# Differential attention in a diffusion block: scores as alternating matmuls on the upper and lower 64 rows, three passes each, keys in two parts

## The chip, the cores and the metric

The kernel runs on one core of a Trainium2 chip. The metric is the device time of one execution in microseconds (us); each version is timed several times and the median is quoted.

## What is computed

The reference is one layer of a diffusion block on 1024 latent tokens with 256 context tokens: an input projection, three parallel branches (differential attention, pooling, windowed attention), their merge, and a feed-forward part. Only the differential attention is touched. It has 4 heads, and each head has two sub-heads `s` with queries and keys of 64 features (q of 1024 tokens, k of 1280):

```python
s = jnp.einsum('bqhsd,bkhsd->bhsqk', qblk, k).astype(jnp.float32) * scale
p = jax.nn.softmax(s, axis=-1)
a = p[:, :, 0] - lam * p[:, :, 1]
return jnp.einsum('bhqk,bkhe->bqhe', a.astype(v.dtype), v)
```

The kernel keeps float32 accuracy by cutting each operand into a high part that fits the matmul's reduced type and a low remainder. A product is then the sum of the products of parts.

## The kernel before

The program is a row of stages with barriers: `prepare`, `project`, `features`, `diff` (the differential attention), `window`, `merge`, `residual`, `ffn_in`, `ffn_out`. The change touches `diff`, and in `features` only the early load of head 0.

`project` leaves, per head, four stacks in DRAM (`stacks_da`), q of sub-head 0, q of sub-head 1, k of sub-head 0, k of sub-head 1, each of 128 rows: 64 rows of high parts above 64 rows of low parts. `load_head` (L776) brings a head on SP's queue with five DMAs: `q_st` and `k_st` as they lie, `k_sw` with its two halves swapped, and `val`. `features` issues it for head 0 (L586), `diff` for the other three.

`diff` runs a hardware loop over two pairs of heads. A turn of the loop (`it`) has 16 tiles of 128 queries (8 for each head of the pair), so there are 32 tiles, and 19 steps, because the tail of a tile's work is done up to three steps later (LAG_TURN 2, LAG_AV 3). PSUM banks 0 to 2 hold the scores of sub-head 0, banks 3 to 5 those of sub-head 1, without a second buffer; banks 6 and 7 form a ring for transposes and products. Every engine has its order written out:

- PE, step i: `scores(i)` (L868), the transposes of the "last" two key blocks of tile i-2, the `products` with the values of tile i-3 (L888), then the transposes "low" and "high" of tile i-2 (L881). In `scores`, sub-head s first waits for `exp_done[s]` of tile i-1, since that exp reads the banks which are now overwritten. Each of its three column pieces (512, 512, 256) takes two matmuls over all 128 rows: q stack by `k_st`, which gives high by high and low by low, and q stack by `k_sw`, which gives the two mixed products. `sc_done[s]` goes up after each sub-head's six.
- DVE (VectorE): `maximum` of sub-head 0 and of sub-head 1 (L981, L982), `combine` of tile i-1 (L996), then the reciprocals, which wait for both exps of tile i.
- ACT (ScalarE): exp of sub-head 0 (L927), `copy_last` (L943, L946), which waits for the products, exp of sub-head 1, two copies "low" and "high" (L934), and a sum of squares (L956). `copy_last` frees the bank into which PE writes the "high" transposes.

Of the kernel before, what the change touches and what calls it, by code (L numbers as in the profile page):

```python
# [34 lines left out]
F32 = mybir.dt.float32  # L35
F32R = mybir.dt.float32r
# [5 lines left out]
P = 128  # L42
D = 1024
SEQ = 1024
CTX = 256
TOK = SEQ + CTX
KC = D // P
TL = SEQ // P
TT = TOK // P
# [5 lines left out]
HD = 64  # L55
# [441 lines left out]
def features(nc, sem, banks, io, keep):  # L497
# [11 lines left out]
    with ExitStack() as ctx:  # L509
        sb = lambda n, s, d=F32: ctx.enter_context(nc.sbuf_tensor(n, s, d))  # L510
# [28 lines left out]
        @block.sync  # L539
        def _(sp):  # L540
            for dst, src in ((pw, io["pool_w"]), (pscale, io["pool_scaleT"]), (badaT, io["b_adaT"]), (ngT, io["norm_gT"])):
                sp.dma_start(dst[:], src).then_inc(small_in, 16)

            def load_w(f, slot):
                sp.wait_ge(w_lo_ready, f - 1)
                sp.dma_start(w_raw[slot][:], io["w_feat"][f]).then_inc(w_in[slot], 16)

            def load_piece(q, slot):
                sp.wait_ge(piece_used, q + 1)
                sp.dma_start(piece[slot][:], io["w_ada"].rearrange("(k p) n -> p k n", p=P)  # L550
                             .rearrange("p k (a n) -> a p k n", n=AC)[2 * D // AC + q]).then_inc(piece_in[slot], 16)

            def store_gate(f):
                for n in range(NH):
                    sp.wait_ge(gst_ready, (f - G) * NH + n + 1)
                    sp.dma_start(gates[f - G][:, n * HALF:(n + 1) * HALF], gst[n][:]).then_inc(gst_out[n], 16)

            for g in range(G):
                if g:
                    sp.wait_ge(pooled, g)  # L560
                sp.dma_start(inv, io["inv_count"][g:g + 1, :].to_broadcast([P, SEQ])).then_inc(inv_in, 16)
                load_w(g + 2, g % 2)
                if g >= 1:
                    sp.wait_ge(yb_ready, g)
                    sp.dma_start(io["yb"][g - 1], yb[:]).then_inc(yb_out, 16)

            def turn(it, pieces, more):
                for j in range(2):
                    f = it * 2 + G + j
                    if more:  # L570
                        load_w(f + 2, j)
                    for q in range(2 * pieces):
                        load_piece((it - 1) * 4 + 2 * j + q, q)
                    store_gate(f)

            load_w(G + 2, 0)
            sp.wait_ge(yb_ready, G)
            sp.dma_start(io["yb"][G - 1], yb[:]).then_inc(yb_out, 16)
            store_gate(G)
            load_w(G + 3, 1)  # L580
            store_gate(G + 1)
            with sp.Fori(1, 1 + A_TURNS) as it:
                turn(it, 1, True)
            with sp.Fori(1 + A_TURNS, TURNS - 1) as it:
                turn(it, 0, True)
            load_head(io, sp, 0, keep["head0"], keep["head0_in"])  # L586
            sp.wait_ge(ada_ready, 1)
            for i in range(2):
                if i:
                    sp.wait_ge(row_used, 2)  # L590
                sp.dma_start(brow, io["b_ada"][0:1, (2 + 3 * i) * D:(3 + 3 * i) * D].to_broadcast([P, D])).then_inc(row_in, 16)
                sp.dma_start(grow, io["norm_g"][1 + 2 * i:2 + 2 * i, :].to_broadcast([P, D])).then_inc(row_in, 16)
            turn(TURNS - 1, 0, False)
            sp.wait_ge(row_used, 3)
            sp.dma_start(io["late_row"], upad[0:1, 0:D]).then_inc(yb_out, 16)
            for j in range(2):
                sp.wait_ge(keep["st_out"][j], keep["st_stored"])
            for n in range(NH):
                sp.wait_ge(gst_out[n], 16 * (3 * KC + 1))
            sp.wait_ge(yb_out, 16 * (G + 1))  # L600
# [174 lines left out]

def load_head(io, sp, h, buffers, landed):  # L776

    q, k, ks, val = buffers
    src = io["stacks_da"][h]
    for dst, s in ((q[:], src[0:2, :, 0:SEQ]), (k[:], src[2:4])):  # L780
        sp.dma_start(dst.bitcast(F32), s.rearrange("s p n -> p s n")).then_inc(landed, 16)
    for a, b in ((0, HD), (HD, 0)):
        sp.dma_start(ks[a:a + HD].bitcast(F32), src[2:4, b:b + HD].rearrange("s p n -> p s n")).then_inc(landed, 16)
    sp.dma_start(val[:], io["vals"][h].rearrange("t p n -> p t n")).then_inc(landed, 16)


def window_buffers(keep):
# [20 lines left out]
def diff(nc, sem, banks, io, keep):  # L808
# [4 lines left out]
    TILES = 2 * TL  # L813
    LAG_TURN, LAG_AV = 2, 3
    COLS = [(0, HALF), (HALF, HALF), (2 * HALF, TOK - 2 * HALF)]
    with ExitStack() as ctx:
        sb = lambda n, s, d=F32: ctx.enter_context(nc.sbuf_tensor(n, s, d))

        heads = [keep["head0"], (sb("q_st1", [P, 2, SEQ], F32R), sb("k_st1", [P, 2, TOK], F32R), sb("k_sw1", [P, 2, TOK], F32R),
                                 sb("val1", [P, TT, P]))]  # L820
        q_st, k_st, k_sw, val = zip(*heads)
        e = [[sb(f"e{b}{s}", [P, TOK]) for s in range(2)] for b in range(2)]
        a = [sb(f"a{b}", [P, TOK]) for b in range(2)]
        at = [sb(f"at{b}", [P, TT, P]) for b in range(2)]
# [7 lines left out]
        sc_done, neg_ready, exp_done = ([sem(f"da_{n}{s}") for s in range(2)] for n in ("sc", "neg", "exp"))  # L832
# [12 lines left out]
        def slot(it, i, what):  # L845

            n = 3 * (i - LAG_TURN) + RING.index(what)
            return n % 2, it * USES + n // 2
# [12 lines left out]
        @block.tensor  # L861
        def _(pe):
            def use(it, i, what):
                b, used = slot(it, i, what)
                pe.wait_ge(free[b], used + 1)
                return b, banks[6 + b]

            def scores(it, i):  # L868
                j, t = i // TL, i % TL
                if t == 0:  # L870
                    pe.wait_ge(head_in[j], 80 * it + 80)
                for s in range(2):
                    pe.wait_ge(exp_done[s], it * TILES + i + 1)
                    q = q_st[j][:, s, t * P:(t + 1) * P]
                    for c, (c0, w) in enumerate(COLS):
                        out = banks[3 * s + c][:, 0:w]
                        pe.matmul(out, q, k_st[j][:, s, c0:c0 + w], start=True, stop=False)
                        mm = pe.matmul(out, q, k_sw[j][:, s, c0:c0 + w], start=False, stop=True)  # L878
                    mm.then_inc(sc_done[s], 1)

            def turn(it, t, i, what):  # L881

                b, bank = use(it, i, what)
                for n, k in enumerate(KEYS[what]):
                    mm = pe.transpose(bank[:, n * P:(n + 1) * P], a[t % 2][:, k * P:(k + 1) * P], ident[:])
                return b, mm

            def products(t, bank):  # L888
                for k in range(TT):
                    mm = pe.matmul(bank[:, 2 * P:3 * P], at[t % 2][:, k, :], val[t // TL][:, k, :], start=(k == 0), stop=(k == TT - 1))  # L890
                return mm

            with pe.Fori(0, 2) as it:
                for i in range(STEPS):
                    t = i - LAG_TURN
                    if i < TILES:
                        scores(it, i)
                    if t >= 0:
                        if t < TILES:
                            pe.wait_ge(a_ready, it * TILES + t + 3)  # L900
                            b, mm = turn(it, t, i, "last")
                        else:
                            b, bank = use(it, i, "last")
                        if t >= 1:
                            for what in ("low", "high"):
                                bb, used = slot(it, i - 1, what)
                                pe.wait_ge(free[bb], used + 2)
                            mm = products(t - 1, banks[6 + b])
                            mm.then_inc(av_done, 1)
                            pe.wait_ge(av_done, it * TILES + t)  # L910
                            pe.sem_inc(turned[b], 1)
                        else:
                            mm.then_inc(turned[b], 1)
                    if 0 <= t < TILES:
                        for what in ("low", "high"):
                            b, mm = turn(it, t, i, what)
                            mm.then_inc(turned[b], 1)
                pe.sem_inc(turned[slot(it, STEPS - 1, "low")[0]], 1)
# [1138 lines left out]
```

## Time and profile before

| | us |
|---|---|
| median of 3 executions | 2089.27 |
| lowest and highest | 2085.03, 2089.52 |
| span of the profiled execution | 2084.4 |
| `diff` in it, first score matmul to last product | 679.0 to about 907 |

The profiled execution is one more execution; its span runs from its first to its last instruction, and no other time of it is given. Times in the trace count from the span's start. A row of the timeline has the start, the duration, engine, line, operation, tiles and shapes, a count where equal instructions are merged, and in brackets the idle time before it and what ended it. The granted clock of TensorE (PEclk) is 1.00 at 2.4 GHz and 0.50 at 1.2 GHz. Matmuls overlap, so their pace is read from start to start and not from their durations. PEld is the weight load, which runs beside the matmuls.

### The profile page before, as it was taken

The numbers are of one execution on the slowest core, as the hardware profiler recorded it, in microseconds if no ns is written. First come the engines' busy times: TensorE is split into PE (matmuls) and PEld (weight loads), VectorE is DVE, ScalarE is ACT, GpSimd is POOL, SyncE is SP. The second block draws the span as 40 slices with busy tenths as digits, with TensorE's granted clock in tenths as the row PEclk, the third lists the DMA queues.
The fourth block names the chain that finished last, engine by engine and source line by source line (L and its number), as shares of the span: only waits on it lengthen the run. The fifth ranks groups of instructions, "written<-read, shape, count | busy, mean of one in ns | idle before, by whom it ended". The sixth has DMA issues, their size and how long they took to land. (4 is left out here: it accounts for less than half of the span.)

```text
span 2084.4 us, 28313 instructions
## 1 busy us (share of the span) xinstructions
PE 1951.4 (94%) x10084; PEld 1665.9 (80%) x10084; DVE 855.8 (41%) x1526; ACT 661.1 (32%) x1218; POOL 390.4 (19%) x209
## 2 busy tenths in 40 slices
PE   6799999999999898979899989799999999989998
PEld 2699998788887787869887878688888888878886
DVE  2755554736531786858673346500000000032322
ACT  2422222122221675755451025411111111132332
POOL 0321120222221000020001212122222222133433
PEclk9799999999999999999899999899999999999999
DMA  9133322266655333220204342211111111143431
GB/s 327 61 100 96 105 82 87 104 189 191 188 155 182 84 84 83 65 81 2 72 0 152 136 164 84 81 41 50 50 50 43 47 50 50 40 152 100 162 111 71
DMA packets 132934, 207.17 MB, mean 99 GB/s; under 512 B 10881, under 2 KB 93441, under 8 KB 132098
## 3 DMA queue, kind: packets, MB, share of 16 engines
q1 hardware_dynamic: 132866, 206.31, 30.4%
q8 instruction: 37, 0.61, 0.1%
q14 instruction: 31, 0.25, 0.0%
HBM read 164.99 MB, written 41.29 MB: 99 GB/s over the span
## 5 line engine op out<-in xcount | busy, mean ns | idle before, releaser
L490 PE MATMUL psum<-h_hi,cut_hi 128*128 128x512 f32 x704 | 275.0, 391 | 6.1 <-DVEq L1716 6.1
L491 PE MATMUL psum<-h_lo,cut_hi 128*128 128x512 f32 x704 | 274.6, 390 | 0.0
L493 PE MATMUL psum<-h_hi,cut_lo 128*128 128x512 f32 x704 | 217.2, 390 | 0.0
L1723 DVE TENSOR_TENSOR f<-psum,i_act 128x512 f32 x44 | 28.4, 687 | 454.7 <-PE psum L493 454.7
L490 PE MATMUL psum<-h_hi,f_hi 128*128 128x512 f32 x448 | 177.7, 397 | 2.3 <-ACTq L668 2.3
L491 PE MATMUL psum<-h_lo,f_hi 128*128 128x512 f32 x448 | 175.9, 393 | 0.0
L1704 POOL TENSOR_TENSOR cut_lo<-stage,cut_hi 128x1024 fp32r<-128x1024 f32 x42 | 100.7, 2397 | 367.5 <-ACT cut_hi L1683 367.5
L76 PE MATMUL psum<-w_hi,h_hi 128*128 128x384 f32 (+1 forms) x464 | 156.7, 338 | 5.7 <-DVE w_lo L431 5.6
L490 PEld LDWEIGHTS psum<-h_hi,cut_hi 128*128 128x128 f32 x704 | 132.6, 188 | 34.0 <-DVEq L1715 6.5
L491 PEld LDWEIGHTS psum<-h_lo,cut_hi 128*128 128x128 f32 x704 | 132.7, 189 | 27.6
L493 PEld LDWEIGHTS psum<-h_hi,cut_lo 128*128 128x128 f32 x704 | 132.5, 188 | 27.7
L78 PE MATMUL psum<-w_hi,h_lo 128*128 128x384 f32 (+1 forms) x464 | 151.8, 327 | 0.0
L77 PE MATMUL psum<-w_lo,h_hi 128*128 128x384 f32 (+1 forms) x464 | 151.7, 327 | 0.0
L76 PE MATMUL psum<-u_hi,uf_hi 128*128 128x512 f32 x352 | 138.3, 393 | 5.9 <-POOL uf_lo L1871 5.6
L493 PE MATMUL psum<-h_hi,f_lo 128*128 128x512 f32 x448 | 138.7, 391 | 0.0
L77 PE MATMUL psum<-u_lo,uf_hi 128*128 128x512 f32 x352 | 137.9, 392 | 0.0
L78 PE MATMUL psum<-u_hi,uf_lo 128*128 128x512 f32 x352 | 137.9, 392 | 0.0
L1888 DVE TENSOR_TENSOR u_lo<-stage,u_hi 128x1024 fp32r<-128x1024 f32 x44 | 58.4, 1330 | 157.6 <-ACT u_hi L1849 157.6
L697 POOL TENSOR_TENSOR f_lo<-f_raw,f_hi 128x1024 fp32r<-128x1024 f32 x26 | 65.2, 2507 | 267.7 <-ACT f_hi L657 267.7
L1871 POOL TENSOR_TENSOR uf_lo<-f,uf_hi 128x512 fp32r<-128x512 f32 x44 | 78.4, 1787 | 156.1 <-ACT uf_hi L1850 156.1
L981 DVE TENSOR_REDUCE mx<-psum 128x1 f32<-128x1280 f32 x64 | 95.2, 1487 | 21.7 <-PE psum L878 19.2
L1683 ACT ACTIVATE cut_hi<-stage 128x1024 fp32r<-128x1024 f32 x42 | 44.6, 1063 | 187.0 <-PE psum L493 187.0
(232 smaller groups left out, 3839.5 us busy)
## 6 DMA issues: line engine op xcount, KB each, us to landing
stage<-in_w_ff SPq DMA_DIRECT2D x44, 512.0 KB, 3.3
stage<-in_w_ffn_out SPq DMA_DIRECT2D x44, 512.0 KB, 3.3
piece<-in_w_ada SPq DMA_DIRECT2D x32, 512.0 KB, 5.6
f_raw<-in_w_feat SPq DMA_DIRECT2D x28, 512.0 KB, 4.3
gates_dram<-gst SPq DMA_DIRECT2D x48, 256.0 KB, 2.1
b_g<-gates_dram SPq DMA_DIRECT2D x8, 1536.0 KB, 7.9
w_raw<-in_w_tok SPq DMA_DIRECT2D x6, 1536.0 KB, 6.7
ada<-in_w_ada SPq DMA_DIRECT2D x8, 1024.0 KB, 11.4
```

The source lines that it names most:

```text
L76: pe.matmul(out, sh, mh, start=first, stop=False)
L77: pe.matmul(out, sh, ml, start=False, stop=False)
L78: return pe.matmul(out, sl, mh, start=False, stop=last)
L490: pe.matmul(out, sh, mh, start=first, stop=False)
L491: pe.matmul(out, sh, ml, start=False, stop=False)
L493: mm = pe.matmul(out, sl, mh, start=False, stop=last)
L697: eng.tensor_tensor(w_lo[slot][:], w_raw[slot][:], w_hi[slot][:].bitcast(F32), ALU.subtract).then_inc(w_lo_ready, 1)
L981: ch.link(v.tensor_reduce(mx[:, s:s + 1], psum[:, 3 * s * HALF:3 * s * HALF + TOK], AX.X, ALU.max))
L1683: act.activation(w_hi[slot][:], w_raw[slot], ACT.Copy).then_inc(w_hi_ready, 1)
L1704: eng.tensor_tensor(w_lo[slot][:], w_raw[slot], w_hi[slot][:].bitcast(F32), ALU.subtract).then_inc(w_lo_ready, 1)
L1871: nc.gpsimd.tensor_tensor(f_lo[j][:], f[:, k, c * HALF:(c + 1) * HALF], f_hi[j][:].bitcast(F32), ALU.subtract).then_inc(f_lo_ready, 1)
L1888: v.tensor_tensor(w_lo[j][:], w_raw[(q + c * FC) % 2][:], w_hi[j][:].bitcast(F32), ALU.subtract)\
```

## The change

The k_sw stack goes. q and k are loaded so that rows 0 to 63 hold sub-head 0 and rows 64 to 127 sub-head 1, and the high and low parts lie side by side in the middle dimension. `load_head` still has five DMAs, each of the q and k ones over 64 rows. A score is now three matmuls of 64 rows (high by high, high by low, low by high; low by low is no longer computed). The two sub-heads alternate from matmul to matmul, each on its own half of the rows and into its own banks. That makes 18 matmuls for a tile in place of 12. Both waits, for `exp_done[0]` and `exp_done[1]` of the tile before, stand ahead of the first of them, and `sc_done[0]` goes up with the last but one, `sc_done[1]` with the last.

```diff
--- before.py
+++ after.py
@@ -583,7 +583,7 @@
                 turn(it, 1, True)
             with sp.Fori(1 + A_TURNS, TURNS - 1) as it:
                 turn(it, 0, True)
-            load_head(io, sp, 0, keep["head0"], keep["head0_in"])
+            load_head(io, sp, 0, head0_buffers(keep), keep["head0_in"])
             sp.wait_ge(ada_ready, 1)
             for i in range(2):
                 if i:
@@ -775,13 +775,19 @@
 
 def load_head(io, sp, h, buffers, landed):
 
-    q, k, ks, val = buffers
-    src = io["stacks_da"][h]
-    for dst, s in ((q[:], src[0:2, :, 0:SEQ]), (k[:], src[2:4])):
-        sp.dma_start(dst.bitcast(F32), s.rearrange("s p n -> p s n")).then_inc(landed, 16)
-    for a, b in ((0, HD), (HD, 0)):
-        sp.dma_start(ks[a:a + HD].bitcast(F32), src[2:4, b:b + HD].rearrange("s p n -> p s n")).then_inc(landed, 16)
+    q, k, val = buffers
+    src = io["stacks_da"][h].rearrange("u (x d) n -> u d x n", x=2)
+    for s in range(2):
+        rows = slice(s * HD, (s + 1) * HD)
+        sp.dma_start(q[rows].bitcast(F32), src[s, :, :, 0:SEQ]).then_inc(landed, 16)
+        sp.dma_start(k[rows].bitcast(F32), src[2 + s]).then_inc(landed, 16)
     sp.dma_start(val[:], io["vals"][h].rearrange("t p n -> p t n")).then_inc(landed, 16)
+
+
+def head0_buffers(keep):
+
+    q, k, ks, val = keep["head0"]
+    return q, k, val
 
 
 def window_buffers(keep):
@@ -813,12 +819,12 @@
     TILES = 2 * TL
     LAG_TURN, LAG_AV = 2, 3
     COLS = [(0, HALF), (HALF, HALF), (2 * HALF, TOK - 2 * HALF)]
+    PARTS = [(0, 0), (0, 1), (1, 0)]
     with ExitStack() as ctx:
         sb = lambda n, s, d=F32: ctx.enter_context(nc.sbuf_tensor(n, s, d))
 
-        heads = [keep["head0"], (sb("q_st1", [P, 2, SEQ], F32R), sb("k_st1", [P, 2, TOK], F32R), sb("k_sw1", [P, 2, TOK], F32R),
-                                 sb("val1", [P, TT, P]))]
-        q_st, k_st, k_sw, val = zip(*heads)
+        heads = [head0_buffers(keep), (sb("q_st1", [P, 2, SEQ], F32R), sb("k_st1", [P, 2, TOK], F32R), sb("val1", [P, TT, P]))]
+        q_st, k_st, val = zip(*heads)
         e = [[sb(f"e{b}{s}", [P, TOK]) for s in range(2)] for b in range(2)]
         a = [sb(f"a{b}", [P, TOK]) for b in range(2)]
         at = [sb(f"at{b}", [P, TT, P]) for b in range(2)]
@@ -871,12 +877,16 @@
                     pe.wait_ge(head_in[j], 80 * it + 80)
                 for s in range(2):
                     pe.wait_ge(exp_done[s], it * TILES + i + 1)
-                    q = q_st[j][:, s, t * P:(t + 1) * P]
-                    for c, (c0, w) in enumerate(COLS):
-                        out = banks[3 * s + c][:, 0:w]
-                        pe.matmul(out, q, k_st[j][:, s, c0:c0 + w], start=True, stop=False)
-                        mm = pe.matmul(out, q, k_sw[j][:, s, c0:c0 + w], start=False, stop=True)
-                    mm.then_inc(sc_done[s], 1)
+
+
+                for c, (c0, w) in enumerate(COLS):
+                    for n, (a, b) in enumerate(PARTS):
+                        for s in range(2):
+                            rows = slice(s * HD, (s + 1) * HD)
+                            mm = pe.matmul(banks[3 * s + c][:, 0:w], q_st[j][rows, a, t * P:(t + 1) * P],
+                                           k_st[j][rows, b, c0:c0 + w], start=n == 0, stop=n == len(PARTS) - 1)
+                            if c == len(COLS) - 1 and n == len(PARTS) - 1:
+                                mm.then_inc(sc_done[s], 1)
 
             def turn(it, t, i, what):
```

## Rows read from the trace of the kernel before

**Rows 1.** The page: the span and TensorE's share of it.

```profile
span 2084.4 us, 28313 instructions
PE 1951.4 (94%) x10084; PEld 1665.9 (80%) x10084; DVE 855.8 (41%) x1526; ACT 661.1 (32%) x1218; POOL 390.4 (19%) x209
```

**Rows 2.** Timeline of PE, one steady step of the attention.

```profile
741.24 0.48 PE L877 MATMUL psum<-k_st,q_st 128*128 128x512 f32 x1
741.56 0.39 PE L878 MATMUL psum<-k_sw,q_st 128*128 128x512 f32 x1
...
742.26 0.28 PE L877 MATMUL psum<-k_st,q_st 128*128 128x256 f32 x1
742.37 0.27 PE L878 MATMUL psum<-k_sw,q_st 128*128 128x256 f32 x1
...
743.51 0.28 PE L878 MATMUL psum<-k_sw,q_st 128*128 128x256 f32 x1
...
743.85 2.40 PE L890 MATMUL psum<-val,at 128*128 128x128 f32 x20
746.40 1.43 PE L885 MATMUL psum<-ident,a 128*128 128x128 f32 x8
747.58 0.48 PE L877 MATMUL psum<-k_st,q_st 128*128 128x512 f32 x1
```

**Rows 3.** Timeline of DVE, the same step.

```profile
742.75 1.49 DVE L981 TENSOR_REDUCE mx<-psum 128x1 f32<-128x1280 f32 x1
...
744.35 1.48 DVE L981 TENSOR_REDUCE mx<-psum 128x1 f32<-128x1280 f32 x1
```

**Rows 4.** Timeline of ACT, the same step.

```profile
744.47 1.33 ACT L927 ACTIVATE e<-psum,neg_m 128x1280 f32<-128x1280 f32 x1 [1.11 <-DVE neg_m L982]
745.70 0.19 ACT L927 ACTIVATION_READ_ACCUMULATOR e<-psum,neg_m 128x1 f32 x1
746.47 0.37 ACT L943 ACTIVATE o<-psum,rec 128x128 f32 x1 [0.58 <-PEq L911]
...
747.00 1.33 ACT L927 ACTIVATE e<-psum,neg_m 128x1280 f32<-128x1280 f32 x1
748.22 0.21 ACT L927 ACTIVATION_READ_ACCUMULATOR e<-psum,neg_m 128x1 f32 x1
```

**Rows 5.** Timeline of ACT: the first and last exp of sub-head 0 in either turn.

```profile
683.25 1.33 ACT L927 ACTIVATE e<-psum,neg_m 128x1280 f32<-128x1280 f32 x1 [0.39 <-DVE neg_m L982]
...
776.19 1.33 ACT L927 ACTIVATE e<-psum,neg_m 128x1280 f32<-128x1280 f32 x1 [1.11 <-DVE neg_m L982]
...
797.41 1.33 ACT L927 ACTIVATE e<-psum,neg_m 128x1280 f32<-128x1280 f32 x1 [0.40 <-DVE neg_m L982]
...
889.88 1.33 ACT L927 ACTIVATE e<-psum,neg_m 128x1280 f32<-128x1280 f32 x1 [1.11 <-DVE neg_m L982]
```

**Rows 6.** Timeline of PE, the first tile of all.

```profile
679.00 0.79 PE L877 MATMUL psum<-k_st,q_st 128*128 128x512 f32 x1 [5.14 <-ACTq L961]
...
680.01 0.63 PE L877 MATMUL psum<-k_st,q_st 128*128 128x512 f32 x1
680.44 0.63 PE L878 MATMUL psum<-k_sw,q_st 128*128 128x512 f32 x1
```

**Rows 7.** Busy time by stretch: columns PE, PEld, DVE, ACT, POOL, PEclk, DMA share, GB/s.

```profile
684.72:690.60 5.88, 4.26 (x12) 3.33 (x12) 4.15 (x8) 2.84 (x4) 0.00 (x0) 0.69 1.04 270
690.60:696.00 5.40, 3.51 (x18) 2.72 (x18) 5.04 (x7) 2.80 (x5) 0.00 (x0) 1.00 0.81 168
798.90:804.20 5.30, 2.83 (x12) 2.08 (x12) 3.60 (x7) 2.84 (x4) 0.00 (x0) 1.00 1.05 289
804.20:809.80 5.60, 4.80 (x18) 3.85 (x18) 5.04 (x7) 2.86 (x5) 0.00 (x0) 0.70 1.06 215
744.47:750.81 6.34, 6.04 (x44) 5.30 (x44) 5.19 (x8) 4.64 (x11) 0.00 (x0) 1.00 0.55 181
```

**Rows 8.** Timeline of DVE, the end of the features stage.

```profile
673.96 1.23 DVE L772 TENSOR_TENSOR upad<-psum,piece 128x1024 f32<-128x1024 f32 x1 [6.12 <-DMA piece<-in_norm_g]
```

## The prediction

> **What bounds the kernel now.** I read the page first: TensorE (PE) is busy for 94% of 2084.4 us [rows 1], so fewer matmul slots look like time saved. The change lies in the attention only, so I then read one steady step of it in the timelines of PE, DVE and ACT. From score start to score start it lasts 747.58 - 741.24 = 6.34 us [rows 2], and PE is busy in 6.04 of these [rows 7]. The twelve score matmuls run from 741.24 to 743.51 by their starts, the products take 2.40 us from 743.85, ACT's copy follows at 746.47 [rows 4], and it frees the bank for the last transposes before the next scores. So PE's own round, through that one copy, sets the step.
>
> A second loop runs beside it, through the score banks: scores, maximum, exp, and then scores again. Sub-head 0 has its maximum at 742.75, sub-head 1 only at 744.35 [rows 3]; exp 0 starts at 744.47 and exp 1 at 747.00 [rows 4]. The next scores of sub-head 0 start at 747.58, while exp 1 is still running: it ends at 748.22 + 0.21 = 748.43. Today this is harmless. PE does the six matmuls of sub-head 0 first (1.15 us), and comes to sub-head 1 at about 748.7, when exp 1 has ended. The stagger of the two sub-heads hides 0.85 us of exp 1.
>
> **The matmuls.** Removed: twelve of 128 rows; added: eighteen of 64 rows. At full clock the pace of 512 columns is 0.23 us (three in 742.26 - 741.56 = 0.70), that of 256 columns 0.11 (742.37 - 742.26), and the first matmul has 0.32 before its second [rows 2]. No row shows a matmul on 64 rows, so I bound the cost from both sides. If the halves don't overlap, eighteen follow one another: the last of sub-head 0 starts at 0.32 + 11 x 0.23 + 4 x 0.115 = 3.31 us. If each pair shares a slot and the weight loads too, it is 0.32 + 5 x 0.23 + 2 x 0.115 = 1.70. Between lies the case in which pairs overlap and loads don't: the twenty product matmuls have only 128 columns and still take 2.40 / 20 = 0.12 us each [rows 2], the pace of a weight load. Two loads then cost 0.23 for every pair, which fits below 512 columns and not below 256, and the last matmul of sub-head 0 starts at 0.32 + 7 x 0.23 = 1.93 us. I take this one: each half has its own rows and its own banks, which speaks for overlap, and 0.12 us for a load is the nearest row.
>
> The Trainium skill, TensorE: Matmul & The Clock Gate, section Part 3: Packing small matmuls, states that matmuls on different row groups run at the same time, starting about 4 ns apart, and that four row tiles of 512 columns gave 3.07 times the rate. No row of this trace shows it. By the 4 ns the sum stays as it is; by 3.07 out of 4 a pair would cost about 1.3 slots, an estimate that adds some 0.4 us a step to it.
>
> From the start of the last matmul of a sub-head to its maximum it is 742.75 - 742.37 = 0.38 us [rows 2, 3]. Call L the time from the first score matmul to the first maximum: 1.51 us now, 1.93 + 0.38 = 2.31 after (2.08 with shared loads, 3.69 in series). All the slots saved are saved for sub-head 1; sub-head 0 gets its scores later than today.
>
> **The wait that is moved.** `exp_done[1]` of the tile before now stands ahead of all scores. Behind it in PE's order are both sub-heads' scores, the transposes and the products; DVE and ACT wait for these. The loop through the banks becomes:
>
> - L = 2.31 to the first maximum;
> - 744.47 - 742.75 = 1.72 to exp 0 [rows 3, 4];
> - 745.70 + 0.19 - 744.47 = 1.42 for exp 0 with its accumulator read [rows 4];
> - 0.55 for `copy_last` ahead of exp 1, from 747.00 - 746.47 = 0.53 and a small step [rows 4];
> - 748.43 - 747.00 = 1.43 for exp 1, and 0.05 to PE, an estimate from the small gaps of these rows.
>
> Together L + 5.17 = 7.48 us, against 6.34. What else could be late? The products end at about 1.93 + 0.11 + 0.34 + 2.40 = 4.8 us after the step's start and their copy could go at 5.0; exp 0 ends at 2.31 + 3.14 = 5.45, so the products have 0.4 us to spare. The second maximum ends, with its scaling, before `copy_last` is over: DVE is 1.60 us behind its first maximum there [rows 3] and exp 1 could start at L + 3.32, against L + 3.69. ACT's copies and squares after exp 1 are done today 1.11 us before the next exp 0 [rows 4], and that exp comes later relative to them after the change.
>
> In the first two periods of each turn there is no `copy_last`, and maximum 1 opens exp 1: L + 1.72 + 1.60 + 1.43 + 0.05, so L + 4.8 = 7.1; the third is about 7.2.
>
> **Sum at full clock.** A turn has 15 periods between its first and last exp 0: 2 x 7.1 + 7.2 + 12 x 7.48 = 111.2 us, against 776.19 - 683.25 = 92.9 and 889.88 - 797.41 = 92.5 [rows 5]. That is 18.3 + 18.7 = 37.0. The first exp of a turn comes later by the 0.8 of L: + 1.6. The tail gains about 0.4 per turn, since exp 1 follows exp 0 after 1.97 in place of 2.53: - 0.8. Sum + 37.8.
>
> **The clock.** The first tile runs at the 1.2 GHz level: 512 columns take 0.43 us and the first matmul 0.6 [rows 6]. In the second turn the clock is full over two steps in which PE is busy for 2.83 of 5.30 us, and then it is at 0.70 in the next stretch [rows 7], with steps of scores alone before it. After the change such steps have 2.0 us of scores in 7.1, less than there. I take four cold scores in the first turn and two in the second. Cold, L is 0.6 + 7 x 0.43 + 0.6 = 4.2, which is 1.9 more: 6 x 1.9 = 11.4, less 1.0, because the first exp 0 of today was already cold (683.25 - 679.00 = 4.25 [rows 5, 6], where I counted 1.51 + 1.72 plus 0.8). Net + 10.4, with 0 and 16 as bounds. In steady steps PE will be busy for some 5.6 of 7.5 us in gaps below 1 us, and 690.60 to 696.00 had 3.51 of 5.40 at clock 1.00 [rows 7], so there I take the full clock.
>
> **The loads.** `k_sw` of 1.28 MB goes from each head. Heads 1 to 3 have tens of us of cover, the attention steps before their first use. Head 0's load stands in the features stage ahead of row loads for which DVE waited 6.12 us at its end [rows 8]; after that wait only about 2.5 us of DVE and a store are left, next to the last gates, which PE's end holds. I take - 0.5, bounds 0 and - 1. No cover is lost, since nothing is added to SP.
>
> Forecast: 37.8 + 10.4 - 0.5 = + 47.7 on a profiled span of 2084.4, so 2132 as a span. It is 4.9 below the median of 2089.27 in the runs shown; the delta is put on the median: 2137 us.
>
> **The rivals.**
>
> 1. The halves don't overlap, so that the change doesn't do what it says. L is 3.69, the step 8.86: 2 x 8.5 + 8.6 + 12 x 8.86 = 131.9 per turn, + 78.7 for both; + 4.4 for the first exps, - 0.8 for tails, + 6 for the colder start: + 88, so 2177 us. For it: not one row shows an overlap. Against it: separate rows, weights and banks.
> 2. The clock sinks in steady steps too, since PE now rests twice in each step. Cold scores give L = 4.2; the products end at 4.2 + 0.5 + 20 x 0.22 = 9.1 and become the late ones; copy, exp 1 and the way back add 2.0: 11.1 us a step, + 3.6 over the forecast. For 24 steps that is + 87: 2224 us, or half, if it comes and goes. Rows 7 speak against it.
> 3. Faster: the joint wait doesn't bind, and PE's round alone sets the step. It would be 6.34 less 0.34 (2.27 us from first to last score start become 1.93), or less 0.55 with shared loads: 26 steps x 0.34 = - 9, so 2080 us. The place is the wait at the head of `scores`; it decides from L + 5.17 < 6.34, so L below 1.17 us. Nine slots of columns alone need 1.70 + 0.38, so only a shorter chain of maxima and exps could bring it, and every link of that is a measured row.
>
> **How the numbers follow.** Forecast 0.65, series 0.19, clock 0.08, faster 0.04, and 0.04 for a result within 0.2%, if small gains elsewhere pay for the wait. Within the forecast the low end has shared loads (- 7) and no cold start (- 10): 2119. The range runs from there to the series case with its start: 2117 to 2180. A measurement of this kernel can tell about 0.2% from no change. Slower by more than that: 0.92; within: 0.04; faster: 0.04.
>
> **What would show it.** Right: steps of 7.3 to 7.6 us between the exps of sub-head 0, the two maxima back to back with the first some 2.3 us after the scores' start, PE waiting for exp 1 ahead of the first score, and pairs of matmuls of the two halves starting together. The first maximum at 3.7 us after the start would show series; matmuls of 0.63 us in mid-turn would show the clock. The prediction is wrong if the next scores start before exp 1 of the tile before has ended, or if the steps of 6.34 us stay.

## The result and the profile after

The changed kernel takes 2124.79 us (median of 4 runs, 2123.81 to 2127.53), the kernel before 2089.11 beside it: 1.0173 times as long, with a 95% interval of 1.0161 to 1.0186, so + 35.7 us. The forecast was 2137, its range 2117 to 2180. The profiled spans are 2123.8 and 2084.4 us, 39.4 apart.

The page of the changed kernel, its head:

```profile
span 2123.8 us, 28729 instructions
PE 1950.4 (92%) x10276; PEld 1663.6 (78%) x10276; DVE 859.3 (40%) x1526; ACT 656.8 (31%) x1218; POOL 390.2 (18%) x209
```

In the sum PE is busy for as long as before [rows 1], 1950 us: the 39 us more of the span are idle time of PE. The steady step tells where most of them are. Timelines of PE, then DVE, then ACT of the changed kernel:

```profile
746.15 0.63 PE L895 MATMUL psum<-ident,a 128*128 128x128 f32 x4
747.18 0.66 PE L895 MATMUL psum<-ident,a 128*128 128x128 f32 x4 [0.40 <-ACT at L956]
748.58 2.03 PE L886 MATMUL psum<-k_st,q_st 64*128 64x512 f32 x18 [0.74 <-ACT e L937]
750.53 0.44 PE L895 MATMUL psum<-ident,a 128*128 128x128 f32 x2
750.81 2.40 PE L900 MATMUL psum<-val,at 128*128 128x128 f32 x20
```

```profile
750.65 1.49 DVE L991 TENSOR_REDUCE mx<-psum 128x1 f32<-128x1280 f32 x1 [1.64 <-PE psum L886]
752.17 0.15 DVE L992 TENSOR_SCALAR neg_m<-mx 128x1 f32<-128x1 f32 x1
752.24 1.48 DVE L991 TENSOR_REDUCE mx<-psum 128x1 f32<-128x1280 f32 x1
```

```profile
745.18 1.33 ACT L937 ACTIVATE e<-psum,neg_m 128x1280 f32<-128x1280 f32 x1 [2.68 <-DVE neg_m L992]
746.40 0.19 ACT L937 ACTIVATION_READ_ACCUMULATOR e<-psum,neg_m 128x1 f32 x1
746.49 0.36 ACT L953 ACTIVATE o<-psum,rec 128x128 f32 x1
...
747.01 1.34 ACT L937 ACTIVATE e<-psum,neg_m 128x1280 f32<-128x1280 f32 x1
748.22 0.22 ACT L937 ACTIVATION_READ_ACCUMULATOR e<-psum,neg_m 128x1 f32 x1
```

All eighteen score matmuls take 750.53 - 748.58 = 1.95 us, against 743.64 - 741.24 = 2.40 for the twelve of before ([rows 2], and the next row of that timeline):

```profile
743.64 0.38 PE L885 MATMUL psum<-ident,a 128*128 128x128 f32 x2
```

The halves do overlap: read one by one, the pairs of 512 columns start 0.23 us apart and those of 256 columns about 0.11, and the second matmul of a pair starts 0.03 to 0.07 us behind the first. But the scores start only when exp 1 has ended, at 748.44 (the bracket: PE idle for 0.74 us, released by ACT's exp), where [rows 2, 4] had sub-head 0 start 0.85 us before that end. The first maximum comes 2.07 us after the start, in place of 1.51 [rows 2, 3]. ACT, which had 0.58 us to wait for the products ahead of its copy [rows 4], now goes from exp 0 to the copy at once: the products are no longer late, the exps are. The steady step is 7.19 us for 6.34.

The exps of sub-head 0 that answer to [rows 5], from ACT's timeline of the changed kernel:

```profile
683.75 1.33 ACT L937 ACTIVATE e<-psum,neg_m 128x1280 f32<-128x1280 f32 x1 [0.39 <-DVE neg_m L992]
...
795.46 1.33 ACT L937 ACTIVATE e<-psum,neg_m 128x1280 f32<-128x1280 f32 x1 [2.65 <-DVE neg_m L992]
...
818.11 1.33 ACT L937 ACTIVATE e<-psum,neg_m 128x1280 f32<-128x1280 f32 x1 [0.40 <-DVE neg_m L992]
...
929.25 1.33 ACT L937 ACTIVATE e<-psum,neg_m 128x1280 f32<-128x1280 f32 x1 [2.65 <-DVE neg_m L992]
```

Against [rows 5]: + 0.5 at the first, + 18.8 in the first turn (111.7 for 92.9), + 1.4 between the turns (22.65 for 21.22), + 18.7 in the second (111.1 for 92.5). That is 39.4, the whole difference of the spans; all stages behind are as long as before. Of a turn's 18.7, about 10 are twelve steady steps, the rest is the first three periods, which answer to [rows 7] (busy time by stretch, columns as there):

```profile
683.75:692.16 8.41, 3.47 (x18) 2.90 (x18) 3.63 (x7) 2.83 (x4) 0.00 (x0) 0.62 1.04 209
692.16:700.67 8.51, 5.05 (x24) 4.06 (x24) 5.10 (x8) 2.84 (x5) 0.00 (x0) 0.60 0.13 33
700.67:709.15 8.48, 5.99 (x39) 5.20 (x40) 5.09 (x8) 3.98 (x7) 0.00 (x0) 0.80 0.00 0
709.15:716.34 7.19, 5.87 (x51) 5.03 (x50) 5.14 (x8) 4.52 (x10) 0.00 (x0) 1.00 0.01 2
```

They take 8.4 to 8.5 us at a mean clock of 0.60 to 0.80. PE has little but scores in the first two (18 and 24 matmuls), and the scores of all three take 3.5 us in place of 1.95.

### The profile page after: what moved, and what is told of

Its sections match the earlier page's. It is cut to its first block and busy times, and to the rows that moved or that the text cites. A ratio compares the mean times of both kernels' runs of the same rounds, so it can differ in the third digit from the quotient of the medians.

```text
span 2123.8 us, 28729 instructions
## 1 busy us (share of the span) xinstructions
PE 1950.4 (92%) x10276; PEld 1663.6 (78%) x10276; DVE 859.3 (40%) x1526; ACT 656.8 (31%) x1218; POOL 390.2 (18%) x209
## 3 DMA queue, kind: packets, MB, share of 16 engines
q1 hardware_dynamic: 131842, 201.06, 29.7%
## 5 line engine op out<-in xcount | busy, mean ns | idle before, releaser
L886 PE MATMUL psum<-k_st,q_st 64*128 64x512 f32 (+1 forms) x576 | 74.5, 405 | 45.4 <-ACT e L937 38.5
L937 ACT ACTIVATE e<-psum,neg_m 128x1280 f32<-128x1280 f32 x64 | 85.2, 1331 | 95.9 <-DVE neg_m L992 95.9
```

Of the source, the lines that this page charges most:

```text
L886: mm = pe.matmul(banks[3 * s + c][:, 0:w], q_st[j][rows, a, t * P:(t + 1) * P], k_st[j][rows, b, c0:c0 + w], start=n == 0, stop=n == len(P ...
L937: act.activation(e[i % 2][s][:], psum[:, 3 * s * HALF:3 * s * HALF + TOK], ACT.Exp, scale=SCALE, bias=neg_m[:, i % 2, s:s + 1], accum_out= ...
```

## The experiments

The theory is that the joint wait ends the stagger of the two sub-heads and hangs the step on a loop through L, both exps and back, L + 5.11 us by the trace of after. Its rival puts the cost into the matmuls of 64 rows, their number or their loads.

**e1_joint_wait**: the kernel before, with only the wait moved.

```diff
                 for s in range(2):
                     pe.wait_ge(exp_done[s], it * TILES + i + 1)
+                for s in range(2):
                     q = q_st[j][:, s, t * P:(t + 1) * P]
```

> The kernel before with one edit: both exp waits stand ahead of sub-head 0's six matmuls (128 rows, two passes, as before). Theory (the joint wait undoes the stagger): in the step of before exp 1 ends 748.43 - 741.24 = 7.19 us after the scores' start, and products, copy and exp 1 ahead of it don't change, so the step goes from 6.34 to about 7.24 us and the run gains 13 us a turn and some for the cold start, + 25 to + 33 us in all. Rival (the narrow matmuls or their loads cost the time, the wait is covered): steps stay at 6.34, + 0 to + 3 us.

Measured: 1.0162 (1.0143 to 1.0182), 2124.0 against 2090.2 us, steps of 7.34 us. PE's timeline of e1_joint_wait:

```profile
748.67 0.47 PE L878 MATMUL psum<-k_st,q_st 128*128 128x512 f32 x1 [0.74 <-ACT e L928]
748.98 0.39 PE L879 MATMUL psum<-k_sw,q_st 128*128 128x512 f32 x1
```

The same bracket as in the changed kernel, with the old matmuls. The wait alone costs + 34 us, a little over the + 25 to + 33 expected and as much as the whole change within the intervals. The rival's + 0 to + 3 is out. The step is 7.34 and not 7.24 because the way from the end of exp 1 to the first score is 748.67 - (748.31 + 0.21) = 0.15 us, by ACT's timeline, for which I had 0.05.

**e2_alternate_old**: the wait moved and the sub-heads alternating, still two passes of 128 rows.

```diff
-                    for c, (c0, w) in enumerate(COLS):
...
+                for c, (c0, w) in enumerate(COLS):
+                    for n, keys in enumerate((k_st[j], k_sw[j])):
+                        for s in range(2):
+                            mm = pe.matmul(banks[3 * s + c][:, 0:w], q_st[j][:, s, t * P:(t + 1) * P],
+                                           keys[:, s, c0:c0 + w], start=n == 0, stop=n == 1)
...
```

> The kernel before with both waits ahead and the two sub-heads alternating, still with twelve matmuls of 128 rows. Theory: the first maximum waits for the eleventh matmul, so L = 2.16 + 0.38 = 2.54 us, and the bank loop, whose rest was 7.18 - 2.07 = 5.11 in the changed kernel, makes steps of 7.65 us; + 45 to + 55 us, so more than the changed kernel's + 36, because here no pair of matmuls overlaps. Rival (the row halves bring nothing): no slower than the changed kernel, steps of 7.2 or below.

Measured: 1.0266 (1.0247 to 1.0284), + 54 us, steps of 7.65 us, the number of the sum L + 5.11; L is 2.54 in its trace too. So alternation by itself delays sub-head 0 and makes it worse than e1_joint_wait; the eighteen matmuls on halves, which overlap, earn back some 19 us of that (1.0266 to 1.0173).

**e3_blocks**: the new matmuls in the old order, nine of sub-head 0 behind its wait, then nine of sub-head 1 behind its own. e4 to e6 share its code, with another LEAD.

```diff
-                for s in range(2):
-                    pe.wait_ge(exp_done[s], it * TILES + i + 1)
...
+                mine = [(c, n) for c in range(len(COLS)) for n in range(len(PARTS))]
+                LEAD = 9
+                pe.wait_ge(exp_done[0], it * TILES + i + 1)
+                for x in range(len(mine) + LEAD):
+                    if x == LEAD:
+                        pe.wait_ge(exp_done[1], it * TILES + i + 1)
+                    for s, y in enumerate((x, x - LEAD)):
+                        if not 0 <= y < len(mine):
+                            continue
...
```

> The changed kernel's eighteen matmuls of 64 rows, but nine of sub-head 0 behind its own wait and then nine of sub-head 1 behind its own, as the order of before. Theory: a matmul of 64 rows alone takes the slot of one with 128 (0.23 us for 512 columns), so the scores take 3.45 us; PE's round sets the step again, 6.34 + 1.15 = 7.5 us; the stagger is back, and the first maximum comes 2.1 us after the start. + 30 to + 40 us. Rival (a 64-row matmul is cheaper by itself, alternating isn't what overlaps them): scores in about 1.9 us, steps near 6.0, - 5 to - 10 us.

Measured: 1.0193 (1.0172 to 1.0214), + 38 us, steps of 7.38. PE's timeline of e3_blocks, one step:

```profile
745.09 1.43 PE L898 MATMUL psum<-ident,a 128*128 128x128 f32 x8
746.44 3.27 PE L889 MATMUL psum<-k_st,q_st 64*128 64x512 f32 x18
749.64 0.44 PE L898 MATMUL psum<-ident,a 128*128 128x128 f32 x2
```

The same eighteen matmuls take 3.20 us here, near the 3.45 expected for eighteen full slots, and 1.95 when they alternate. A matmul of 64 rows by itself takes nearly the slot of one of 128 rows, and the gain is in the pairing alone. The stagger is back here, but PE's round is longer: ACT waits 0.87 us for the products ahead of its copy.

**e4_lead3, e5_lead2, e6_lead4**: alternating, with sub-head 0 ahead by three, two or four matmuls that need only exp 0 (LEAD = 3, 2, 4).

> The changed kernel, but sub-head 0 leads by three matmuls (its first 512 columns), which wait for exp 0 alone; the wait for exp 1 comes then, and the rest alternates in pairs, sub-head 1 three behind. Theory: exp 1 is awaited 0.78 us into the scores, L is 2.30, so the bank loop gives 2.30 + 5.11 - 0.78 = 6.63 us; PE's round 6.34 + 0.12 = 6.46 lies below it. Steps of 6.6 us, + 8 to + 15 us, so two thirds of the loss of + 36 is given back by order alone. Rival (the cost is in the 64-row matmuls and their loads): steps stay near 7.2, + 30 or more.

> As e4_lead3, with sub-head 0 two matmuls ahead. In e4_lead3 the step was 6.83 us, set by PE's round and not by the bank loop. Theory: the wait for exp 1 now stands 0.55 us into the scores, L about 2.26, so the bank loop gives 2.26 + 5.11 - 0.55 = 6.82; PE's round loses two slots of 0.115 and is about 6.6. Steps of 6.8 us, + 18 to + 24 us, no better than lead 3, with PE now waiting for exp 1 inside the scores. Rival (only the number of slots on PE counts): 6.6 and + 10 to + 15.

> As e4_lead3, with sub-head 0 four matmuls ahead. Theory: PE's round has 0.23 us more than with lead 3, so steps of 7.06 us; the bank loop (2.26 + 5.11 - 1.01 = 6.36) doesn't bind. + 26 to + 32 us. Rival (the bank loop still binds in lead 3, so more lead helps): 6.6 us or less, + 12 to + 16.

| | ratio | 95% interval | steady step, us |
|---|---|---|---|
| changed kernel (no lead) | 1.0173 | 1.0161 to 1.0186 | 7.19 |
| e5_lead2 | 1.0110 | 1.0093 to 1.0126 | 6.83 |
| e4_lead3 | 1.0108 | 1.0090 to 1.0127 | 6.84 |
| e6_lead4 | 1.0118 | 1.0101 to 1.0134 | 6.84 |
| e3_blocks (lead of nine) | 1.0193 | 1.0172 to 1.0214 | 7.38 |

Order alone, with the same matmuls and loads, gives back 13 us, so the theory stands; but two of the three expectations missed. Lead 3 cost + 21 us and not + 8 to + 15, and lead 4 + 24 and not + 26 to + 32, no worse than lead 3 within the intervals. Only lead 2 came as expected, with its step of 6.83 set by the bank loop: ACT goes from exp 0 to the copy at once there, while in lead 3 and 4 it waits 0.15 and 0.32 us for PE's products. I had PE's round too low for lead 3 (6.46) and too high for lead 4 (7.06). The timeline of e4_lead3 shows it:

```profile
747.37 1.43 PE L898 MATMUL psum<-ident,a 128*128 128x128 f32 x8
748.73 2.73 PE L889 MATMUL psum<-k_st,q_st 64*128 64x512 f32 x18
751.39 0.44 PE L898 MATMUL psum<-ident,a 128*128 128x128 f32 x2
751.66 1.06 PE L903 MATMUL psum<-val,at 128*128 128x128 f32 x8
```

Its copy of that step starts at 747.45, so from the copy to the first score it is 1.28 us, where [rows 2, 4] have 747.58 - 746.47 = 1.11; transposes to products take 0.27 where they took 0.21; and the scores take 751.39 - 748.73 = 2.66 where they took 2.40. That is 0.17 + 0.06 + 0.26 = 0.49 on top of 6.34, the step of 6.83; I had counted 0.12. e3_blocks has the same 1.28. The scores take 2.66 us in lead 4 as well. In lead 3 a load among them waits 0.20 us for exp 1; in lead 4 none waits, but one more matmul at either end runs without a partner. None of the three comes near the 6.34 us of before.

**e9_dummy128, e10_dummy64**: is the missing time the way from 128-row to 64-row matmuls? The kernel before gets one small matmul ahead of sub-head 0's scores, whose output they overwrite, on 128 rows (control) or on 64.

```diff
                     q = q_st[j][:, s, t * P:(t + 1) * P]
+                    if s == 0:
+                        pe.matmul(banks[0][:, 0:P], k_st[j][:, 0, 0:P], k_st[j][:, 0, 0:P], start=True, stop=True)
```

(e10_dummy64 has `k_st[j][0:HD, 0, 0:P]` in both places.)

> The kernel before with one added matmul of 128 rows and 128 columns ahead of sub-head 0's scores, whose output is overwritten by them. It is the control of e10_dummy64: its slot is about 0.12 us, PE sets the step, so steps of 6.45 us and + 2 to + 5 us.

> As e9_dummy128, but the added matmul is on 64 rows, with 128-row work on either side. In e3_blocks to e6_lead4 the way from copy_last to the first 64-row score was 1.28 us against 1.11 before, and from the transposes to the products 0.28 against 0.22. Theory (going from 128-row to 64-row matmuls and back costs PE time): steps 0.2 to 0.3 us longer than in e9_dummy128, 6.65 to 6.75, + 9 to + 14 us. Rival (that 0.17 us belongs to the first score's load or its wait, not to the change of rows): the same steps as e9_dummy128.

Measured: e9_dummy128 1.0019 (1.0003 to 1.0034), steps of 6.45 us, as expected; e10_dummy64 1.0094 (1.0066 to 1.0121), + 20 us, steps of 6.80; both lie above what was expected, + 9 to + 14 us and 6.65 to 6.75. The step is the firmer measure: 31 periods by 0.35 us are 11 us, while the two ratios lie some 16 us apart. PE's timeline of e9_dummy128:

```profile
750.44 0.31 PE L876 MATMUL psum<-k_st 128*128 128x128 f32 x1
750.58 0.44 PE L879 MATMUL psum<-k_st,q_st 128*128 128x512 f32 x1
750.86 0.39 PE L880 MATMUL psum<-k_sw,q_st 128*128 128x512 f32 x1
```

and of e10_dummy64:

```profile
749.88 0.32 PE L876 MATMUL psum<-k_st 64*128 64x128 f32 x1
750.13 0.50 PE L879 MATMUL psum<-k_st,q_st 128*128 128x512 f32 x1
750.47 0.39 PE L880 MATMUL psum<-k_sw,q_st 128*128 128x512 f32 x1
```

The copies ahead start at 749.33 and 748.60, so the added matmul comes 1.11 and 1.28 us later: 0.17 to go in. Behind it the second score matmul is at 0.42 and at 0.59 us: 0.17 to come out. Together 0.35 us a step, shown by the step itself. The Trainium skill, TensorEngine Tiling (Array Packing), section Tiling Modes, says that a change of tiling mode drains TensorE. The 0.17 us on either side of the 64-row matmul agree with that; no run shows the drain itself. In the changed kernel the way in hides in the wait for exp 1: scores follow the end of exp 1 after 748.58 - 748.44 = 0.14 us, in e1_joint_wait with its 128-row matmuls after 0.15. With a lead it doesn't hide: of the 0.37 us by which e4_lead3's step missed, 0.17 are the way in and 0.06 lie on the way out, and the other 0.14 are in the score block.

**e7_warm, e8_warm64**: ten added matmuls behind the scores of steps 1 and 2, on 128 rows in e7, on the upper 64 in e8.

```diff
                     if i < TILES:
                         scores(it, i)
+                    if i in (1, 2):
+                        for n in range(10):
+                            pe.matmul(banks[7][:, 0:HALF], k_st[0][:, 0, 0:P], k_st[0][:, 0, 0:HALF], start=True, stop=True)
```

> The changed kernel with ten added matmuls of 128x512 behind the scores of steps 1 and 2 of each turn, whose output into a bank unused at that time nobody reads: they keep PE busy where it otherwise rests for 4.9 us. Theory (the 8.5 us of the first periods are 7.0 plus scores at 1.2 GHz): the second and third periods of each turn fall from 8.51, 8.48 and 8.50, 7.88 to 7.0 to 7.3 us, the first stays near 8.5, the steady steps at 7.18; 4 to 6 us off the changed kernel, so + 29 to + 32 us on the kernel before. Rival (these steps are long for another reason, the loads or the first uses): no period changes, + 35 or more.

> As e7_warm, but the ten added matmuls of steps 1 and 2 use only the upper 64 rows. In e3_blocks the granted clock stayed at 0.50 for over 25 us in which PE ran 64-row matmuls of one half at a time nearly without a break, while in e7_warm it rose within ten matmuls of 128 rows. Theory (matmuls on one half of the rows don't bring the clock back, PE's busy time is not what counts): the added ones stay at 0.43 us each, and the second and third periods stay at 8.4 to 8.6 us and near 8. Rival (any matmul does): as e7_warm, periods of 6.94 us.

e7_warm: 1.0148 (1.0131 to 1.0166), 2119.6 us, 5 below the changed kernel. The two intervals just overlap, but the periods between exps of sub-head 0 leave no doubt: 8.51, 6.94, 6.95 us in the first turn, 8.50, 6.94, 6.93 in the second. PE's timeline of e7_warm:

```profile
684.74 3.57 PE L886 MATMUL psum<-k_st,q_st 64*128 64x512 f32 x18 [4.88 <-ACT e L940]
688.24 3.33 PE L910 MATMUL psum<-k_st 128*128 128x512 f32 x10
693.25 1.99 PE L886 MATMUL psum<-k_st,q_st 64*128 64x512 f32 x18 [1.68 <-ACT e L940]
```

So the long periods are scores at 1.2 GHz (3.50 us to the next matmul in place of 1.92), and work on PE in the gaps removes that. e8_warm64 was timed only once, 2125.7 us, its periods 8.50, 8.50, 6.95 and 8.51, 8.50, 6.95. Neither its theory nor its rival holds: the clock rose during the first ten half-height matmuls, but after 1.9 us without a matmul the next scores ran at 0.50; the second ten ran at full clock, and so did the scores behind them. The first of these, columns as in [rows 7]:

```profile
693.20:695.00 1.80, 1.80 (x8) 1.09 (x6) 1.77 (x3) 1.24 (x2) 0.00 (x0) 0.92 1.01 251
695.00:696.90 1.90, 0.00 (x1) 0.02 (x1) 1.77 (x4) 1.60 (x4) 0.00 (x0) 1.00 0.00 0
696.90:700.20 3.30, 3.29 (x18) 2.90 (x19) 0.41 (x2) 0.00 (x0) 0.00 (x0) 0.50 0.01 2
```

## Why the prediction was right, and where it was off

- **The place.** The moved wait and the loop through the banks were as forecast: the loop was to be L + 5.17 and is L + 5.11. Its links agree but for two small ones that nearly cancel: the copy starts 1.31 us after exp 0 and not 1.42, and the way from exp 1 to PE is 0.14 and not 0.05. e1_joint_wait shows that the wait is enough by itself, though there the products, and not exp 0, hold the copy: ACT waits 0.61 us for them.
- **L.** I took 2.31 us, with the loads of a pair one after the other; it is 2.07, the case of shared loads (2.08) that was the low bound. The nearest row, 0.12 us for a load of products on 128 rows, misled: the eighteen loads on alternating halves start within 1.7 us, and the pairs of 256 columns follow one another at 0.11 us, two loads in each. PEld's timeline of the changed kernel:

```profile
748.55 1.85 PEld L886 LDWEIGHTS psum<-k_st,q_st 64*128 64x128 f32 x18 [0.95 <-issue]
```

So the steady step is 7.19 us, just below the 7.3 to 7.6 named as the sign of being right. 24 steps by 0.29 us, 0.24 of it from L, are 7 of the 12 us between 2137 and 2124.8. Another 4 are no error of the sum: it gave + 47.7 for the spans, which differ by 39.4, and was then put on the median, and the medians differ by 35.7 only. The 3.07 of 4 that the prediction quotes from the Trainium skill, TensorE: Matmul & The Clock Gate, section Part 3: Packing small matmuls, is for four tiles; the two halves here did better, two matmuls of 512 columns share a slot whole. The second starts 0.03 to 0.07 us behind the first, and not the 4 ns quoted there.
- **The clock.** Right in kind, and e7_warm shows it. The cold L is 3.55 us, from 692.16 - 686.89 less 1.72, not 4.2, because pairs share their slots there too. The four cold scores of the first turn came as counted; in the second turn a third was cold in part (2.92 us at 838.27) besides the two counted. The twenty products at 799.83 in the tail of the first turn were mostly cold as well, 3.86 us in place of 2.47, which I had not foreseen: the stretch between the turns grew by 1.4 us, where the forecast had 0.8 - 0.4 = 0.4.
- **The loads.** The first score matmul starts at 678.46, 0.54 us earlier than in [rows 6]; forecast 0.5. That the two agree is luck: in the seven runs that share the changed kernel's code up to there it starts anywhere from 676.30 (e3_blocks) to 680.08 us (e8_warm64), so no single pair of traces can show 0.5 us.
- **The rivals.** Series: out, by 1.95 us against 3.20 in e3_blocks. A low clock in steady steps: out, the clock is 1.00 there. Faster: its point of decision, L below 1.17 us, was never near. Its 2080 us was too low besides, because it had no price for changing rows: e10_dummy64 puts 0.35 us on it, about all that the shorter scores would have saved.
- **Slips of the working.** They change nothing. `k_sw` is 1.31 MB a head and not 1.28 (the DMA queue moved 206.31 MB before and 201.06 MB after, four heads apart); the + 78.7 of the series rival is 78.4 by its own numbers; the low end, 2137 less 7 and 10, is 2120, where the text has 2119 and the range 2117.

No version here beats the kernel before. That the lead versions stay 1.1% above it is explained by their steps and their cold first periods; a second set of score banks, which would free the change from its wait, would be six banks more than the eight that the kernel uses already, and wasn't tried.

## What to carry to other kernels

Matmuls paired on two halves of the array finish together and need their outputs' banks free together, so two streams that were staggered to hide each other's softmax become one; before pairing, draw the loop from the banks through their readers and back, and put the pair's time into it. Letting one stream lead by a few matmuls brings part of the stagger back, here 13 of 36 us. The overlap paid for the third pass in PE's own time (1.95 us against 2.40), but not on the loop that sets the step, which waits for the first sub-head alone (L 2.07 against 1.51). Price the way in and out of half-height matmuls, and what the new idle time does to the clock.

## What the runs showed of the hardware

- Two 64-row matmuls on different halves share one slot, loads included: eighteen in 1.95 us, where the same in blocks take 3.20 (e3_blocks).
- A change between 128-row and 64-row matmuls costs 0.17 us each way (e10_dummy64 against e9_dummy128).
- In e3_blocks the granted clock stayed at 0.50 (1.2 GHz) while PE was busy without a break, with half-height matmuls, one half at a time, and 2.4 us of transposes, and came up only with the products on 128 rows. Why e8_warm64 got it up with such matmuls and e3_blocks didn't is open. Its stretches:

```profile
692.00:699.00 7.00, 7.00 (x27) 5.61 (x26) 5.31 (x8) 3.25 (x8) 0.00 (x0) 0.50 0.00 1
699.00:706.00 7.00, 7.00 (x27) 5.94 (x27) 4.03 (x7) 2.36 (x4) 0.00 (x0) 0.50 0.00 0
706.00:713.00 7.00, 6.71 (x43) 5.54 (x43) 3.04 (x4) 3.21 (x8) 0.00 (x0) 0.93 0.01 2
```
